# Dealing the depthwise convolution's taps over the attention heads of a two-model block

## The reference, cut to what matters

```python
px = hx @ w_in[i]                        # hx: 256 tokens; hc: 256 tokens of context
k_x = apply_rope_2(rmsnorm(k_x, k_norm_g[i]), cos, sin)      # 8 heads, 2 maps of 64
...
s = jnp.einsum('bqhcd,bkhcd->bhcqk', qi, keys) * scale       # diff_attention
p = jax.nn.softmax(s, axis=-1)
w = p[:, :, 0] - lam * p[:, :, 1]
...
z = a * jax.nn.sigmoid(g)                                    # conformer_conv, width 512
z = lax.conv_general_dilated(z, w_dw[:, None, :], ...,       # CONV_K = 31, depthwise, centred
                             feature_group_count=CONV_WIDTH) + b_dw
return jax.nn.silu(layernorm(z, ln_g, ln_b))
```

## Time and profile before

| | |
|---|---|
| median of 3 runs | 2333.69 us (2329.54 to 2333.79) |
| the profiled execution's own time | 2330.94 us |
| its span | 2329.1 us |
| TensorE's mean granted clock | 0.991 |
| busy: PE, DVE, ACT | 2247.1, 1544.8, 1082.7 us |

### The profile page before, as it was taken

One profiled execution on the slowest core, in us unless ns is written; L12 is line 12 of the kernel. 1 busy time (PEld: TensorE's weight loads), 2 busy tenths in 40 slices (PEclk: granted clock), 3 DMA queues, 4 the chain that ended last, 5 costly groups with the idle time before them and its releaser, 6 DMA issues.

```text
span 2329.1 us, 34905 instructions
## 1 busy us (share of the span) xinstructions
PE 2247.1 (96%) x13410; PEld 1869.9 (80%) x13410; DVE 1544.8 (66%) x2639; ACT 1082.7 (46%) x2070; POOL 33.4 (1%) x40
## 2 busy tenths in 40 slices
PE   8999999999899999989999999999999999989999
PEld 6658878888857898877777888888788887888988
DVE  5454777575656767578884455766754788767776
ACT  4453422223545555555566524422323765675543
POOL 0300000000100000000000000000000000000000
PEclk9999999999899999999999999999999999999999
DMA  8452467554365555311112232346652222254554
GB/s 315 159 191 73 154 213 268 178 181 135 107 238 181 195 179 174 105 58 61 46 55 73 75 116 73 138 157 212 216 182 91 91 91 75 80 163 148 192 185 138
DMA packets 95316, 335.44 MB, mean 144 GB/s; under 512 B 10672, under 2 KB 12848, under 8 KB 95024
## 3 DMA queue, kind: packets, MB, share of 16 engines
q1 hardware_dynamic: 95152, 333.21, 42.4%
HBM read 332.12 MB, written 1.05 MB: 143 GB/s over the span
## 4 chain that ended last, share of the span: by engine, by line
PE 81%; DVE 10%; ACT 5%; issue 3%; DMA 1%; SPq 0%; ACTq 0%; DVEq 0%
PE out L1507 19%; PE out L1509 19%; PE out L1508 19%; PE out L1501 7%; PE out L1505 3%; DVE w_lo L1909 2%; DVE stage L2270 2%; PE sc L1573 1%; PE pt L1582 1%; ACT w_hi L1639 1%; PE out L1434 1%; DMA raw<-stream 1%; ACT e_t L1802 1%; PE aux L1394 1%; PE pv L1598 1%
## 5 line engine op out<-in xcount | busy, mean ns | idle before, releaser
L1507 PE MATMUL out<-act,w_lo 128*128 128x512 f32 (+1 forms) x1816 | 648.4, 357 | 8.7 <-DVE w_lo L1909 2.9
L1639 ACT CAST w_hi<-raw 128x1024 fp32r<-128x1024 f32 (+2 forms) x444 | 453.8, 1024 | 431.3 <-PE out L1509 268.8
L1509 PE MATMUL out<-act,w_hi 128*128 128x512 f32 (+1 forms) x1816 | 637.4, 351 | 0.0
L1508 PE MATMUL out<-act,w_hi 128*128 128x512 f32 (+1 forms) x1816 | 637.0, 351 | 0.0
L1909 DVE TENSOR_TENSOR w_lo<-raw,w_hi 128x1024 fp32r<-128x1024 f32 (+2 forms) x444 | 528.3, 1192 | 123.0 <-ACT w_hi L1639 122.2
L1507 PEld LDWEIGHTS out<-act,w_lo 128*128 128x128 f32 x1816 | 345.2, 190 | 64.2 <-issue 12.9
L1509 PEld LDWEIGHTS out<-act,w_hi 128*128 128x128 f32 x1816 | 344.6, 190 | 45.9
L1508 PEld LDWEIGHTS out<-act,w_hi 128*128 128x128 f32 x1816 | 345.1, 190 | 43.5 <-issue 0.2
L1507 PE MATMUL out<-mix,w_lo 128*128 128x512 f32 (+1 forms) x734 | 261.5, 356 | 3.2 <-DVE mix L1931 2.2
L1508 PE MATMUL out<-mix,w_hi 128*128 128x512 f32 (+1 forms) x734 | 260.2, 354 | 0.0
L1509 PE MATMUL out<-mix,w_hi 128*128 128x512 f32 (+1 forms) x734 | 260.1, 354 | 0.0
(11 more groups left out here) (291 smaller groups left out, 2844.9 us busy)
## 6 DMA issues: line engine op xcount, KB each, us to landing
raw<-stream SPq DMA_DIRECT2D x604, 512.0 KB, 3.6
raw<-stream SPq DMA_DIRECT2D x16, 384.0 KB, 3.1
raw<-stream SPq DMA_DIRECT2D x16, 256.0 KB, 2.7
x<-xin SPq DMA_DIRECT2D x4, 512.0 KB, 5.3
consts<-const SPq DMA_DIRECT2D x1, 1088.0 KB, 7.1
x<-ctx SPq DMA_DIRECT2D x1, 1024.0 KB, 6.0
out<-x SPq DMA_DIRECT2D x8, 128.0 KB, 1.7
vecs<-vec SPq DMA_DIRECT2D x1, 287.0 KB, 9.0
```

Source lines behind the costliest of these rows:

```text
L1507: nc.tensor.matmul(ps, wl, xh, start=(k == 0), stop=False)
L1508: nc.tensor.matmul(ps, wh, xl, start=False, stop=False)
L1509: ins = nc.tensor.matmul(ps, wh, xh, start=False, stop=(k == s.nk - 1))
L1639: nc.scalar.copy(w_hi[:, number % HL, 0:n], raw[:, place[number] % RAW, 0:n]).then_inc(S["hi_ready"], 1)
```

## The change

The taps are dealt by head: 24 are given to the groups of each of heads 0 and 1, 6 to those of each of heads 2 to 6, in even shares over the head's groups (6 groups in layer 2, 4 in layer 3), and what is left to those of head 7. Each rotation takes one tap where it took three. The lines on `ada_left` change too, but `ada_head`, from which it is filled, is empty in both calls of `layer_second`, so they issue nothing in either kernel. The number of taps stays 124 a layer.

```diff
-UNITS_IN = (1, 2, 2, 2, 2, 2)
+TAPS_IN = (24, 24, 6, 6, 6, 6, 6)
...
-        def taps_due(slots, head):
+        def taps_due(head, part, parts):
 
-            left = 4 * CONV_K - sum(taps_done) - 2 * 3 * max(0, 6 - head)
-            return max(0, -(-left // slots))
+            if head == 7:
+                return -(-(4 * CONV_K - sum(taps_done)) // (parts - part))
+            share = TAPS_IN[head]
+            return (part + 1) * share // parts - part * share // parts
...
-                qk_turn(held["k", h], lambda: conv_taps(3))
+                qk_turn(held["k", h], lambda: conv_taps(1))
...
-                held["qr", h] = query_finish(held["q", h], lambda: conv_taps(3))
+                held["qr", h] = query_finish(held["q", h], lambda: conv_taps(1))
...
-                slots = (8 - h) * len(groups) - j
-                g.append(lambda slots=slots, h=h: conv_taps(taps_due(slots, h)))
+                g.append(lambda h=h, j=j, parts=len(groups): conv_taps(taps_due(h, j, parts)))
```

More of the change, by code:

```diff
@@ L1074, in layer_second @@
             for j, g in enumerate(groups):
-                slots = (8 - h) * len(groups) - j
-                g.append(lambda slots=slots, h=h: conv_taps(taps_due(slots, h)))
[L1077 to L1081, removed]
+                g.append(lambda h=h, j=j, parts=len(groups): conv_taps(taps_due(h, j, parts)))
+                if ada_left and h > 1:
+                    g.append(lambda a=ada_left.pop(0): ada(*a, psum="pt"))
             attend(its, [lambda g=g: [f() for f in g] for g in groups])
```

## The result

The changed kernel takes 2338.4 us (median of 20 runs, 2334.55 to 2344.82) against 2333.64 for the kernel before (20 runs). The ratio is 1.0024, 95% interval 1.0017 to 1.0031, or +5.6 us with +4.0 to +7.2 (the medians lie 4.8 us apart). It is slower by a little, as forecast (2338.5). Its profiled execution took 2338.8 us with a span of 2337.0, 7.9 us over the span before.

A forecast was written before the change was run, and what follows sets the result against it. PE was busy nearly throughout, waiting for DVE's N in a maximum, E, cast, w_lo, N loop. Layer 2 +3.45 and +0.8 for half speed, layer 3 +0.9, gave about +5.2 us; stated 2338.5 us, range 2332 to 2344.

The forecast's parts named there:

- The loop's taps, heads 0 and 1: Layer 2: extra taps ahead of N and of the maximum lie in the three-engine loop; with (2,0), +11.75 us together.
- new half-speed stretches: Layer 2, behind the longer waits at (0,2), (1,0), (1,1) and (2,0): +0.8 us, as those behind the first two hide.
- The clock rival: Half-speed stretches behind four long waits in layer 2 each cost their full 1.7 us: +11.2, 2344.5 us; chance 0.12.
- Rotations at 0: Two taps fewer at each rotation only make DVE wait for ACT's cast: 0, at most 1.3 us a place.
- Heads 2 to 6 of layer 2: Fewer taps in the loop cut PE's waits: -6.5 us in heads 3 to 6, -0.66 at (2,2), -1.7 of clock; -8.9.
- The last head of layer 2: Head 7: 27 more taps, 18 us, mostly covered by DVE's 27.4 us of idle time: +0.6 us.
- as long as before within 1 us: Sign to look for in the changed kernel's profile: the length of layer 2's head 7 stays within 1 us.
- Layer 3: Heads 0 and 1 +1.4 us, heads 2 to 6 -2.7, head 7 with the convolution's norm +2.2: together +0.9 us.
- Idle VectorE taking the early taps in: Heads 0 and 1: idle VectorE absorbs the added taps, so their cost is 0: -8.8 us, 2325; chance 0.08.
- No change through the rotations: An earlier cast makes the rotations' cut give 1.3 us at three places, -4: sum +1.2, 2335 us; chance 0.27 in all.
- my sign of being wrong: Prediction wrong if T in heads 0 and 1 waits no longer than now, or the clock falls in more than four places.

The follow-up runs named there:

- the layer-2-only run: The changed kernel with the new dealing in layer 2 alone, layer 3 dealt as before the change: 2339.12 us, ratio 1.0023 to the kernel before.
- the second experiment: The changed kernel with three taps at each rotation, 12 in the groups of each of heads 0 and 1, 22 in the last head: 2319.06 us, ratio 0.9937.
- the run with the opening moved: The second experiment with the opening's three taps moved ahead of its second value block: 2317.5 us, ratio 0.9931.
- the fastest one: The run with the opening moved, with four taps at each rotation of layer 2 and 6 in each of its heads' groups: 2310.54 us, ratio 0.9901.

## Why the prediction was right, and where its steps were not

The number was right, 2338.4 for 2338.5, and in part by luck. The terms sum to +5.2 us and the two traces differ by 7.9; what is over is mostly the 2.7 us behind the product, for which the sum has no term. The medians differ by only 4.8, and the trace of the kernel before is the only one of 13 without half speed there, so it may stand for a lucky execution; one trace can't show that. Inside the sum, 1.0 us too much for heads 0 to 2 stands against 1.3 too little for the last head. The steps:

- **The loop's taps, heads 0 and 1: right in size, wrong in what it is made of.** Heads 0 to 2 together grew by 10.9 us; my terms gave 11.75 - 0.66 + 0.8 = 11.9. The distances between the T came out term by term, to 0.1 us, and the row from 12 to 24 taps shows each tap paying 0.5 to 0.6 us. (1,1) waits 1.85 us, just under the 2 to 3.5 that I had put as its sign. But I had 0.8 us for new half-speed stretches and waits of 3 us at (0,2) and (1,0); measured are 5.5 us of extra busy PE and waits of 2.90 and 2.17. Most slow matmuls lie inside what would have been waits for N and cost little of their own there, as T of (1,0) and (1,1) show in the layer-2-only run. The clock rival saw the stretches and priced all of them in full. It is not refuted for the whole program: the mean granted clock is 0.9906 over 27 executions of the kernel before and 0.9888 over the 20 of the changed one, by estimate 4.5 us more of clock, and the medians can't tell how much of that hid in waits.
- **Rotations at 0: right in layer 2 (0.1 us), wrong in layer 3.** "Two taps fewer there make DVE wait for ACT and give nothing" took layer 2's rows for both layers. In layer 3 the cut was worth 1.9 us (2.5 in heads 0 and 1, less what heads 2 to 6 gave back), since the 24 taps of heads 0 and 1 had used up VectorE's wait. With the cut, the two waits at the key's norm there sum to 1.6 us; I had put +1.4 on them.
- **Heads 2 to 6 of layer 2: right.** Heads 3 to 6 gave 7.7 us for 8.2 forecast (-6.5 and -1.7), at clock 1.00 and 29.04 us a head.
- **The last head of layer 2: under-sized.** +0.6 forecast, +1.9 measured, and the runs put 28 taps past its knee, which lies between 22 and 28. The sign on record, "as long as before within 1 us", failed. The PE wait that I had followed as covered is there, 1.73 us for L2248.
- **Layer 3: +0.9 forecast, +0.7 measured**; its parts, cut at the maxima, are +3.5, -4.0 and +1.1, where I had +1.4, -2.7 and +2.2. So the sum is right and none of its three windows is. About 1.3 us of the first two is only the cut: 15 matmuls more fall into the first window and 10 fewer into the second. PE's idle time fell from 2.7 to 0.1 us in heads 2 to 6, as forecast; the tail was over-sized by 1.1.
- **The rivals.** Idle VectorE taking the early taps in: dead, by T at (1,0) and by the row of doses from 12 taps on. No change through the rotations: in layer 3 alone. The clock: my sign of being wrong was a fall in more than four places, and it fell in four of layer 2's heads and once at the product, so this sign decides nothing. Its stretches shift times by 1 to 3 us between executions of one and the same dealing, as in the layer-2-only run, and the 2.7 us behind the product belong here.

What stays open is what decides where a half-speed stretch falls. Head 2 of layer 2 took 30.3 us in the second experiment and 31.9 in the run with the opening moved, with the same taps around it, and the product began at half speed in 7 of 13 traces. The wait ahead seems to have a part in it, without deciding it alone. Around T of (0,0) there is half speed in all ten traces where it waits 2.75 us or more, and in none of the three where it waits 2.35 or less; with a wait of 1.46 or 1.47 at (2,0) the clock fell in two of four.

## What to carry to other kernels

Before moving filler work, sort its places by what stands behind each: work inside the loop that the other engines wait for costs most of its duration at once (0.4 to 0.6 us of 0.66 here), while work ahead of an instruction that waits for a third engine is free up to that wait and not beyond. The change under study emptied free places and filled dear ones in heads 0 and 1 (13.0 us in layer 2), which its relief of the dear places in heads 2 to 6 (9.8 us) did not pay for; filling every free place to its knee or just past it (three or four at a rotation, some 20 in the last head, three in the opening) and leaving one tap at each place in the loop gave -1.0%. A place is free only as long as the dealing elsewhere leaves its cover, so it is priced again for each layer and load.

## What the runs showed of the hardware

- A VectorE instruction that waits by semaphore for the one right ahead of it starts 0.13 us later than one that doesn't (four taps 3.11 us against 2.73).
- After a wait of some microseconds TensorE sometimes runs at 1.2 GHz for several microseconds: behind one and the same wait of 3.24 us it made 29 or 30 matmuls in 6 us in the changed kernel and in the layer-2-only run, 38 in the fastest one, and 50 in the kernel before. When such a stretch lies inside a loop that VectorE bounds, it costs little (12.46 against 12.45 us from T to T, with waits of 0.76 and 3.45 us in place of 2.17 and 1.85). Where PE itself is the bound it is paid nearly in full (23.01 against 19.82 us from T of (0,0) to T of (0,1)).
